# A product's first weight slots take the three token tiles that are normed and are held for the last one

## The reference

```python
for i in range(DEPTH):                       # DEPTH = 2, ALPHA = 4 ** 0.25
    m = diff_attention(h, ...) if i % 2 == 0 else short_gated_conv(h, ...)
    h = layer_norm(ALPHA * h + m, ln1_g[i], ln1_b[i])
    h = layer_norm(ALPHA * h + swiglu(h, ffn_w_gate[i], ffn_w_up[i], ffn_w_down[i]),
                   ln2_g[i], ln2_b[i])
# swiglu: (silu(h @ w_gate) * (h @ w_up)) @ w_down, inner width 2816
# short_gated_conv: b, c, x = split(h @ w_in); y = conv3(c * x); (b * y) @ w_out
# third block: z = rms_norm(h) * g; q, k, v, ... = split(z @ w_in_2)
```

## Time and profile before

| | us |
|---|---|
| runs shown | 2309.69, 2314.73, 2315.29 |
| median | 2314.73 |
| profiled execution | 2321.09 |
| its span, first to last instruction | 2319.3 |

### The profile page before, as it was taken

How to read it: one execution, slowest core, us unless ns; L and a number is a source line. 1 busy time by engine, 2 the same in 40 slices (tenths; PEclk the granted TensorE clock), 3 DMA queues, 4 the chain that set the end, 5 groups by cost and what they waited for, 6 DMA issues and landing times.

```text
span 2319.3 us, 29119 instructions
## 1 busy us (share of the span) xinstructions
PE 2043.1 (88%) x10614; PEld 1446.2 (62%) x10615; DVE 673.4 (29%) x1145; ACT 590.3 (25%) x987; POOL 676.1 (29%) x383
## 2 busy tenths in 40 slices
PE   8987889999989998999998989998894887777784
PEld 7864768888878876888886856675683322222221
DVE  2348630110052243111007486123537100000002
ACT  2136323332212222333221124544421000000000
POOL 4421134444614433444451412221240000000000
PEclk9988989999999998999998989998897899999997
DMA  7311023333312323333240412220116799999996
GB/s 209 109 55 37 19 91 99 93 97 100 120 53 82 109 82 101 98 99 92 99 130 19 138 46 64 64 64 0 55 61 254 285 426 426 426 427 426 425 422 245
DMA packets 155402, 362.38 MB, mean 156 GB/s; under 512 B 16671, under 2 KB 88991, under 8 KB 130752
## 3 DMA queue, kind: packets, MB, share of 16 engines
q1 hardware_dynamic: 142880, 341.35, 40.0%
q10 hardware_dynamic: 7664, 11.64, 1.9%
q0 software_dynamic: 4784, 8.40, 1.0%
HBM read 355.58 MB, written 14.68 MB: 160 GB/s over the span
## 4 chain that ended last, share of the span: by engine, by line
PE 68%; DMA 17%; DVE 11%; issue 2%; ACT 1%; POOL 1%; SPq 0%; DVEq 0%; POOLq 0%; ACTq 0%
PE ps L1755 19%; PE ps L1756 19%; PE ps L1757 19%; DMA wpair<-l_expert 15%; PE ps L2186 5%; PE ps L2117 1%; DVE hres L1131 1%; DVE qkm L1406 1%; PE ps L2052 1%; DVE nmax L1209 1%; PE ps L2074 1%; PE ps L2098 1%; DVE attn L1219 1%; DVE ratio L1216 1%; POOL wlo L981 1%
## 5 line engine op out<-in xcount | busy, mean ns | idle before, releaser
L981 POOL TENSOR_TENSOR wlo<-wraw,whi 128x1024 fp32r<-128x1024 f32 (+2 forms) x244 | 571.7, 2347 | 997.1 <-ACT whi L615 996.6
L1755 PE MATMUL ps<-xhi,whi 128*128 128x512 f32 x1152 | 457.1, 397 | 6.4 <-DVE xlo L1110 2.7
L1756 PE MATMUL ps<-xlo,whi 128*128 128x512 f32 x1152 | 453.3, 394 | 0.0
L1757 PE MATMUL ps<-xhi,wlo 128*128 128x512 f32 x1152 | 453.1, 393 | 0.0
L615 ACT CAST whi<-wraw 128x1024 fp32r<-128x1024 f32 (+2 forms) x244 | 245.9, 1014 | 635.9 <-PE ps L1757 601.0
L2186 PE MATMUL ps<-wpair,mx 128*32 128x512 f32 (+1 forms) x2048 | 242.3, 618 | 85.4 <-DMA wpair<-l_expert 84.1
L1755 PEld LDWEIGHTS ps<-xhi,whi 128*128 128x128 f32 x1152 | 219.6, 191 | 57.2 <-issue 11.9
L1757 PEld LDWEIGHTS ps<-xhi,wlo 128*128 128x128 f32 x1152 | 219.2, 190 | 46.3
L1756 PEld LDWEIGHTS ps<-xlo,whi 128*128 128x128 f32 x1152 | 219.5, 191 | 45.3
L2186 PEld LDWEIGHTS ps<-wpair,mx 128*32 128x32 f32 x2048 | 72.4, 113 | 254.3 <-issue 254.2
L1064 POOL COPY nowi<-idx 128x1 uint32 (+1 forms) x33 | 6.1, 186 | 479.4 <-DVE ybuf L1727 429.9
(11 more groups left out here) (403 smaller groups left out, 2394.9 us busy)
## 6 DMA issues: line engine op xcount, KB each, us to landing
wpair<-l_expert SPq DMA_DIRECT2D x192, 1024.0 KB, 25.3
wraw<-ffn_w_gate SPq DMA_DIRECT2D x88, 256.0 KB, 2.8
wraw<-ffn_w_up SPq DMA_DIRECT2D x88, 256.0 KB, 3.0
wraw<-ffn_w_down SPq DMA_DIRECT2D x44, 512.0 KB, 3.5
wraw<-w_in SPq DMA_DIRECT2D x36, 512.0 KB, 3.6
wraw<-attn_w_qkv SPq DMA_DIRECT2D x24, 512.0 KB, 8.2
wraw<-conv_w_in SPq DMA_DIRECT2D x96, 128.0 KB, 2.2
wraw<-attn_w_o SPq DMA_DIRECT2D x8, 512.0 KB, 3.5
```

The lines of the kernel that those rows point to most:

```text
L981: pool.tensor_tensor(l, wraw[:, s, :, 0:cols], h.bitcast(F32), ALU.subtract).then_inc(w_lo, 1)
L1755: pe.matmul(dst, ahi, bhi, start=start, stop=False)
L1756: pe.matmul(dst, ahi, blo, start=False, stop=False)
L1757: return pe.matmul(dst, alo, bhi, start=False, stop=stop)
```

## The change

`row_sums` gets a switch `hold`. With it the last tile is neither transposed nor waited for at its end; the next product does that. It begins with `held_slots`: a first slot for the three tiles that are split (early), then the transposes of the last tile, one more slot for the three tiles, and then both slots again for the last tile (late), each handed back only then. In `feature_group` early passes move 384 columns and late ones 128, so that there are twice as many passes for these two slots (2 x 24 more, or 2 x 18 with three banks). In `token_group`, where a tile is the stationary side, the passes stay as they are and three slots are held. The tile that comes last has to lie outside the banks that the product fills, so a second sequence, `ROWS_LAST` = (2, 3, 1, 0), is used at the first down product and at the convolution output. And `middle` grows by one step: from 4 to 5, and from 6 to 7 behind the second feed-forward. The first group of each product now stands ahead of the loop over the others. The last `row_sums`, in the third block, stays as it is.

```diff
@@ -62,7 +62,7 @@
-CONV_ORDER = (2, 3, 0, 1)
+ROWS_FIRST, ROWS_LAST = (0, 1, 2, 3), (2, 3, 1, 0)
@@ -761,7 +761,7 @@
-            def ffn(next_split, kinds=(0,)):
+            def ffn(next_split, kinds=(0,), order=ROWS_FIRST):
@@ -776,11 +776,11 @@
-                norm_tail(next_split, kinds)
+                norm_tail(next_split, kinds, order)
-            ffn(lambda: split(cols=3 * P, dmas=3, behind=2 * RING))
+            ffn(lambda: split(cols=3 * P, dmas=3, behind=2 * RING), order=ROWS_LAST)
@@ -793,7 +793,7 @@
-            norm_tail(lambda: split(dmas=2, behind=2 * RING), order=CONV_ORDER)
+            norm_tail(lambda: split(dmas=2, behind=2 * RING), order=ROWS_LAST)
@@ -1277,7 +1277,7 @@
-            def ffn(rest=ln_rest):
+            def ffn(rest=ln_rest, order=ROWS_FIRST):
@@ -1286,9 +1286,9 @@
-                norm_stage(FC, ln_half, rest)
-            ffn()
+                norm_stage(FC, ln_half, rest, order=order)
+            ffn(order=ROWS_LAST)
@@ -1308,7 +1308,7 @@
-            norm_stage(DC, ln_half, ln_rest, order=CONV_ORDER)
+            norm_stage(DC, ln_half, ln_rest, order=ROWS_LAST)
@@ -1773,10 +1773,42 @@
-            def token_group(cols=BANKF, chunks=DC, between=None):
+            def held_slots(held, ahead, three_tiles, last_tile):
+                order, source = held
+                for u in range(ahead + 1):
+                    if u == ahead:
+                        turn_normed(order[3], source)
+                    pair_ready(u)
+                    three_tiles(u, (pair.mod(RING) + u) % RING)
+                for u in range(ahead + 1):
+                    pe.wait_ge(xt_lo, xlow.now - (1 if u < 2 else 0))
+                    last_tile(u, (pair.mod(RING) + u) % RING).then_inc(w_used, 1)
+                pair.add(ahead + 1)
+                return ahead + 1
+            def token_group(cols=BANKF, chunks=DC, between=None, held=None):
 
                 par = free.mod(2)
-                for u in range(chunks // 2):
+                done = 0
+                if held:
+                    order = held[0]
+                    def products(t, u, s):
+                        tok = slice(t * P, (t + 1) * P)
+                        for c in range(2):
+                            k = 2 * u + c
+                            mm = three(ps[:, 4 * par + t, 0:cols], xhi[:, k, tok], xlo[:, k, tok],
+                                       whi[:, s, c, 0:cols], wlo[:, s, c, 0:cols], k == 0, k == chunks - 1)
+                        return mm
+                    def three_tiles(u, s):
+                        for n, t in enumerate(order[:3]):
+                            pe.wait_ge(xt_lo, xlow.now - (4 if n < 2 else 2))
+                            products(t, u, s)
+                    done = held_slots(held, 2, three_tiles, lambda u, s: products(order[3], u, s))
+                for u in range(done, chunks // 2):
...
@@ -1792,12 +1824,29 @@
-            def feature_group(banks, chunks=DC, first=0, between=None):
+            def feature_group(banks, chunks=DC, first=0, between=None, held=None):
 
                 par = free.mod(2)
                 if free.first + free.n >= 2:
                     pe.wait_ge(acc_free, free.now - 1)
-                for u in range(chunks // 2):
+                done = 0
+                if held:
+                    last = held[0][3]
+                    assert last in (0, 3) and last // 2 != par
+                    early, late = (slice(P, SEQ), slice(0, P)) if last == 0 else (slice(0, 3 * P), slice(3 * P, SEQ))
+                    def products(u, s, tok, opens):
+                        for c in range(2):
+                            k = 2 * u + c
+                            for b in range(banks):
+                                f = slice(b * P, (b + 1) * P)
+                                mm = three(ps[:, 4 * par + b, tok], whi[:, s, c, f], wlo[:, s, c, f],
+                                           xhi[:, k, tok], xlo[:, k, tok], opens and k == 0, False)
+                        return mm
+                    pe.wait_ge(xt_lo, xlow.now - 2)
+                    done = held_slots(held, 1, lambda u, s: products(u, s, early, True), lambda u, s: products(u, s, late, False))
+                for u in range(done, chunks // 2):
...
@@ -1814,14 +1863,15 @@
-            def ffn(source=None, middle=RING):
-                groups(pe, FC // 2, {pair: RING, free: 1}, lambda g: feature_group(4))
+            def ffn(held, source=None, middle=5, order=ROWS_FIRST):
+                feature_group(4, held=held)
+                groups(pe, FC // 2 - 1, {pair: RING, free: 1}, lambda g: feature_group(4))
                 base = klo.now
-                row_sums(hhi, hlo, FC, list(zip(down_hi, down_lo)), source, middle=middle,
+                row_sums(hhi, hlo, FC, list(zip(down_hi, down_lo)), source, middle=middle, order=order, hold=True,
                          ready=lambda k, t: pe.wait_ge(k_lo, base + k // 2 + 1))
-            def row_sums(ahi, alo, chunks, extra, source=None, ready=None, halves=(1, 0), order=(0, 1, 2, 3), middle=RING, turn_next=None):
+            def row_sums(ahi, alo, chunks, extra, source=None, ready=None, halves=(1, 0), order=ROWS_FIRST, middle=5, turn_next=None, hold=False):
...
@@ -1879,8 +1929,10 @@
                 pair.add(tail)
-                turn_normed(order[3], source)
-                pe.wait_ge(xt_lo, xlow.add(2 * TILES) - 1)
+                xlow.add(2 * TILES)
+                if not hold:
+                    turn_normed(order[3], source)
+                    pe.wait_ge(xt_lo, xlow.now - 1)
@@ -1971,25 +2023,26 @@
             turn_o(0)
-            row_sums(xhi, xlo, DC, list(zip(wo_hi, wo_lo)), halves=(0, 1), turn_next=turn_o,
+            row_sums(xhi, xlo, DC, list(zip(wo_hi, wo_lo)), halves=(0, 1), turn_next=turn_o, hold=True,
                      ready=lambda k, t: pe.wait_ge(ol_ready, 2 * t + k // 4 + 1))
-            ffn()
-            groups(pe, DC, {pair: RING, free: 1}, lambda g: feature_group(3))
+            ffn((ROWS_FIRST, None), order=ROWS_LAST)
+            feature_group(3, held=(ROWS_LAST, None))
+            groups(pe, DC - 1, {pair: RING, free: 1}, lambda g: feature_group(3))
             base = klo.now
-            row_sums(yhi, ylo, DC, list(zip(cout_hi, cout_lo)), order=CONV_ORDER,
+            row_sums(yhi, ylo, DC, list(zip(cout_hi, cout_lo)), order=ROWS_LAST, hold=True,
                      ready=lambda k, t: pe.wait_ge(k_lo, base + k + 2))
             klo.add(DC)
             normed = lambda t: scr[:, t % 2, :]
-            ffn(normed, middle=6)
-            def token_cols(cols):
+            ffn((ROWS_LAST, None), normed, middle=7)
+            def token_cols(cols, held=None):
                 if free.first + free.n >= 2:
                     pe.wait_ge(acc_free, free.now - 1)
-                token_group(cols)
+                token_group(cols, held=held)
                 free.add()
 
-            token_cols(QW)
+            token_cols(QW, (ROWS_FIRST, normed))
             token_cols(2 * KVW)
```

## The result

| kernel | runs shown, us | median | ratio of the two, 95% interval |
|---|---|---|---|
| before | 2314.73, 2309.69, 2315.29, 2307.92 | 2312.21 | |
| changed | 2284.88, 2288.89, 2281.02, 2280.22 | 2282.95 | 0.9879 [0.9857, 0.9901] |

The change makes the kernel 29.3 us faster by these medians. The forecast was 2281.5 us from a gain of 33.2 us. Beside further runs of the kernel before on two other chips the changed kernel had medians of 2281.94 and 2280.64, which are 32.7 and 34.8 us less. The profiled execution of the changed kernel is the one of 2284.88 us, its span 2283.0 us; times in its rows are microseconds from the start of that span.

The account below looks back on a forecast made before the run. TensorE, busy 88% of the span, was taken as the bound, held up at four joints by VectorE's norm. Gains of 6.3 + 8.4 + 5.7 + 12.8 = 33.2 us off the 2314.7 median gave 2281.5 us, range 2272.5 to 2297.

Parts of the forecast that it names:

- four joints: Places where a product summed by token rows hands over to the next; gaps of 7.2, 7.2, 7.2 and 10.3 us.
- A: Handover from the attention output to the first feed-forward; forecast gain 6.3 us.
- B: Handover from the first feed-forward's down product to the convolution's input product; forecast gain 8.4 us.
- C: Handover from the convolution output to the second feed-forward; forecast gain 5.7 us.
- D: Handover from the second feed-forward's down product to the query columns; forecast gain 12.8 us, last tile's norm nearly all covered.
- Late passes: At A to C, 132 passes of 128 columns with a full weight load each, taken at 0.12 us.
- Rivals 1, 2 and 4: Narrow passes cost 0.067 us, 2274.5 (chance 0.13); 0.227, 2295.6 (0.15); or 0.427 at half clock, 2322 (0.03).
- Early passes: At A to C, first-slot passes of 384 columns at 0.173 us, covering VectorE's norm of the last tile, 4.3 us.
- third tile's hole: TensorE waiting for the third tile's norm; transposes one step later save 1.4 us per joint, 1.6 more at B.
- Hand-back of slots: Weight slots returned later: costed at nothing at A to C, 0.2 us at the key columns after D.
- Rival 3: Holes around last tile's transposes lower the clock at B and D, or key columns start 2 us late: 2288, chance 0.12.
- Rival 5: Early passes wait because the third tile's split is late; an early slot lost everywhere leaves 17 us, 2298; chance 0.03.

Follow-up runs that it names:

- second trace of the kernel before: The kernel before, unedited, profiled again beside the step alone and the hold alone; the profiled execution ran in 2309.99 us, median 2316.47 us.
- run on widths: Changed kernel with passes of whole groups in both feed-forwards cut in two along the tokens, in four ways, to measure pass distances; ran once, 2360.62 us.
- hold alone: Changed kernel with the third tile's transposes back where they were before; 2288.86 against 2316.47 us for the kernel before, ratio 0.9888.
- second run of the changed kernel: Changed kernel, unedited, run again on another chip; 2281.94 against 2314.63 us for the kernel before, ratio 0.9856.

## Why the prediction was right, step by step

**The bound.** TensorE waited at the four joints for VectorE's norm, and taking those waits away took the time away: the pieces fell by 34.0 us where the forecast had 33.2, the three medians by 29.3, 32.7 and 34.8. The mechanism was right. The sum was less exact than these numbers look. It was worked out on one trace of the kernel before, and against that trace the changed kernel's pieces fell by 36.3: 15.4 on A and B (forecast 14.7), 8.9 on C (5.7) and 11.9 on D (12.6). The second trace of the kernel before had fewer slow passes and brings the mean down to 34.0, which is luck for the forecast.

**Late passes.** Forecast 0.12 us with bounds of 0.067 and 0.227; measured 0.112 at A to C in all three runs of the changed kernel, and 0.110 to 0.112 in the run on widths. 132 times 0.008 is 1.1 us to the good, 0.7 of it at A and B, which is what they gave beyond the forecast. The floor that the 48-wide passes of the earlier trace rows suggested is there and is the same from 64 to 192 columns. By the Trainium skill (TensorE: Matmul & The Clock Gate, LDWEIGHTS) a load of 128 columns takes 107 ns; the measured distance is 3 to 5 ns above. The 81 ns of the same page's section on the back-to-back issue gap do not hold for passes of this number form with a load each: the late passes of 128 columns, and those of 64 in the run on widths, are 0.11 us apart. That the load is what sets the floor is not shown (see the run on widths). Rivals 1, 2 and 4 fall with this: none of 0.067, 0.227 and 0.427 stands in any late stretch.

**Early passes.** Forecast 0.173 from a line between two widths, measured 0.173 to 0.175. They covered the chain of the norm at A and C entirely; at B 0.98 us of waiting was left where the forecast had 1.2.

**The clock behind the third tile's hole.** At B the restart at the full clock was forecast and came in all three runs. At A and C the slow passes were left in the sum. At C they were gone in all three runs of the changed kernel and at A in one. That is the mis-sized term of C: forecast 5.7, by the pieces 8.2 against the mean of the two runs of before (379.1 to 370.9), 8.9 against the first. The forecast kept them for a hole of about 3.5 us, between a row with 4.9 us and slow passes and one with 2.5 us and none; the later runs show that such a hole goes either way.

**D.** Forecast 12.8 less the 0.2 of the key columns, measured 11.9 (64.5 to 52.6). What failed is "nearly all covered": less than 0.5 us of waiting was to be left before the last tile's transposes, and there were 2.23, 2.25 and 2.25. The timeline of the changed kernel, TensorE's restart and the last row-sum pass, then VectorE's chain and the transposes, answers the earlier trace rows:

```profile
1233.79 0.48 PE L1755 MATMUL ps<-hhi 128*128 128x512 f32 x1
...
1235.03 0.39 PE L1757 MATMUL ps<-hhi,hlo 128*128 128x512 f32 x1
...
1236.26 1.42 DVE L1110 TENSOR_TENSOR xlo<-ps,xhi 128x512 fp32r<-128x512 f32 x2
1237.71 0.69 DVE L1116 SCALAR_TENSOR_TENSOR hres<-hres,ps 128x512 f32<-128x512 f32 x1
...
1239.40 1.99 DVE L1126 SCALAR_TENSOR_TENSOR hres<-hres,mv,gb 128x1024 f32<-128x1024 f32 x1
...
1245.86 1.44 PE L1772 MATMUL ps<-ident,scr 128*128 128x128 f32 x8 [2.23 <-DVE scr L1321]
```

The six passes behind the restart ran at the full clock, so T came at 1235.3, but VectorE was still at the third tile's split and began the last half at 1237.71, 2.4 us behind T where the forecast had 0.9. These 1.5 us are time that the full clock gave TensorE and that VectorE could not use; they cost nothing beside the forecast, since VectorE began 16.4 us behind the second tile's transposes, as forecast. The other 0.7 us of the wait are lost: L1126, 1.28 us elsewhere (307.04 at A), took 1.99 here, since it began at 1239.40 and GpSimd split weights until 1240.29. The forecast had taken the length of the norm from the kernel before, where this operation began when the splits were over. With the hold alone it took 1.28 us too. So the 0.8 us that the forecast gave the later step at D came and were lost again, and that is what D lacks of its 12.6.

**Hand-back of slots.** Costed at nothing at A to C, and no pass waits for weights there. The key columns waited 0.45 us for GpSimd where 0.2 was forecast, and the product behind them 0.74 us where it had been 1.21; the second run of the changed kernel had 0.50 and 0.74, the third none and 1.41:

```profile
1261.39 0.35 PE L1755 MATMUL ps<-whi,xhi 128*128 128x256 f32 x1 [0.45 <-POOL wlo L981]
...
1273.86 0.47 PE L1755 MATMUL ps<-xhi,whi 128*128 128x512 f32 x1 [0.74 <-POOL wlo L981]
```

**The other rivals.** Rival 3 had the clock fall behind the last tile's transposes. In the three runs of the changed kernel it did not; in five of the other kernels with the same wait at D it did (below), and in the four of them that are in the table D took 1.4 to 2.0 us more. The rival is real in kind, at D, and not at B. Rival 5 did not come: the early passes waited nowhere for the third tile's split in the changed kernel, though one step later they do, by 0.7 to 1.0 us.

## What to carry to other kernels

Where a product waits for the last tile's norm, begin it on the tiles that are ready, with enough slots held to cover the norm and with the cut where both parts stay wide. A part of 192 columns or fewer costs 0.11 us all the same, so a cut costs 0.059 us per pass at 128 columns and 0.012 at 256. How few slots are enough is open. Let the early part need only what is done long before, or a wait that one removes by moving a step comes back as a wait for that step's result. And compare traces piece by piece between fixed points, since the far end of the kernel moved by 10 us from run to run and hid differences of 3.
